# One product of 512 columns for the high part of a stationary weight tile, and the sum of its halves at the eviction

## The reference

```python
# first block: depthwise causal convolution over time (width 4) on 512 of the projected columns
qk = causal_dwconv(jnp.concatenate([mq, mk], axis=-1), conv_w[l], conv_b[l])
...
# first block, MLP (1024 -> 4096 -> 1024)
u = jnp.square(jax.nn.relu(h @ w_up[l]))
x = x + rmsnorm(u @ w_down[l], norm_mlp_post[l])
...
# second block, feed-forward of each of its two layers (1024 -> 2 x 2816 -> 1024)
def conv_ffn(h, w_up, conv_w, conv_b, w_down):
    u = h @ w_up
    up = jnp.pad(u, ((0, 0), (CONV_WIDTH_2 - 1, 0), (0, 0)))
    uc = conv_b + sum(conv_w[j] * up[:, j:j + S] for j in range(CONV_WIDTH_2))
    gate, val = uc[..., :D_FF_2], uc[..., D_FF_2:]
    return (jax.nn.silu(gate) * val) @ w_down
```

## Time and profile before

| | |
|---|---|
| median of 3 runs | 1218.11 us (1217.97 to 1219.54) |
| span of the profiled execution, first to last instruction | 1216.8 us |
| mean granted clock of PE in it | 0.973 |
| busy share of PE, PEld, DVE, ACT | 94%, 83%, 62%, 54% |
| weights and other data moved | 183.91 MB, mean 151 GB/s |

### The profile page before, as it was taken

The page is one execution under the profiler, slowest core; times in us unless marked ns, Lnnn a source line. Parts: engine busy times, 40 slices in busy tenths (PEclk is TensorE's granted clock), DMA queues, the critical chain, the costliest instruction groups (busy, mean ns, idle before and its releaser), DMA issues.

```text
span 1216.8 us, 19433 instructions
## 1 busy us (share of the span) xinstructions
PE 1144.5 (94%) x6808; PEld 1014.1 (83%) x6808; DVE 759.6 (62%) x1336; ACT 663.0 (54%) x1124; POOL 8.5 (1%) x11
## 2 busy tenths in 40 slices
PE   6998779999979999999999899999898988999998
PEld 4886678989968888988898799999787777999997
DVE  4667655555546766466654666776665745677666
ACT  5364454444456566465564655555655646555554
POOL 1000100000000000000000000000000000000000
PEclk9998789999999999999999999999999998999999
DMA  8552135666626554055622456555552514555562
GB/s 302 140 172 70 53 114 176 181 188 186 191 87 204 165 185 139 15 172 161 205 69 67 124 174 190 183 171 181 156 173 85 163 64 138 170 179 171 190 204 90
DMA packets 85283, 183.91 MB, mean 151 GB/s; under 512 B 6640, under 2 KB 6896, under 8 KB 84976
## 3 DMA queue, kind: packets, MB, share of 16 engines
q1 hardware_dynamic: 85232, 183.26, 48.2%
HBM read 182.19 MB, written 1.05 MB: 151 GB/s over the span
## 4 chain that ended last, share of the span: by engine, by line
PE 85%; DVE 6%; ACT 5%; issue 3%; DMA 0%; SPq 0%; DVEq 0%; ACTq 0%
PE ps L646 10%; PE ps L647 10%; PE ps L648 10%; PE ps L624 9%; PE ps L626 9%; PE ps L625 9%; PE ps L701 5%; PE ps L702 5%; PE ps L703 5%; PE ps L762 3%; PE ps L742 3%; PE ps L750 2%; DVE w_lo L1351 1%; ACT u L991 1%; PE ps L774 1%
## 5 line engine op out<-in xcount | busy, mean ns | idle before, releaser
L1351 DVE TENSOR_TENSOR w_lo<-w_stage,w_hi 128x1024 fp32r<-128x1024 f32 x336 | 404.1, 1222 | 263.7 <-ACT w_hi L967 263.6
L967 ACT ACTIVATE w_hi<-w_stage 128x1024 fp32r<-128x1024 f32 x336 | 350.0, 1057 | 323.4 <-PE ps L648 165.8
L646 PE MATMUL ps<-aT_hi,w_hi 128*128 128x256 f32 x992 | 285.5, 288 | 10.4 <-DVE aT_lo L1364 3.6
L647 PE MATMUL ps<-aT_lo,w_hi 128*128 128x256 f32 x992 | 284.2, 286 | 0.0
L648 PE MATMUL ps<-aT_hi,w_lo 128*128 128x256 f32 x992 | 284.1, 286 | 0.0
L624 PE MATMUL ps<-w_hi,aT_hi 128*128 128x512 f32 x512 | 205.8, 402 | 2.3 <-DVE aT_lo L1364 2.3
L646 PEld LDWEIGHTS ps<-aT_hi,w_hi 128*128 128x128 f32 x992 | 194.1, 196 | 14.3 <-issue 8.0
L626 PE MATMUL ps<-w_hi,aT_lo 128*128 128x512 f32 x512 | 202.4, 395 | 0.0
L625 PE MATMUL ps<-w_lo,aT_hi 128*128 128x512 f32 x512 | 202.2, 395 | 0.0
L647 PEld LDWEIGHTS ps<-aT_lo,w_hi 128*128 128x128 f32 x992 | 194.0, 196 | 1.0
L648 PEld LDWEIGHTS ps<-aT_hi,w_lo 128*128 128x128 f32 x992 | 193.9, 195 | 0.0
(11 more groups left out here) (173 smaller groups left out, 1151.4 us busy)
## 6 DMA issues: line engine op xcount, KB each, us to landing
w_stage<-in_ffn_w_up SPq DMA_DIRECT2D x88, 512.0 KB, 4.5
w_stage<-in_a_w_qkv SPq DMA_DIRECT2D x72, 512.0 KB, 4.3
w_stage<-in_ffn_w_down SPq DMA_DIRECT2D x44, 512.0 KB, 3.7
w_stage<-in_w_up SPq DMA_DIRECT2D x32, 512.0 KB, 4.3
w_stage<-in_w_down SPq DMA_DIRECT2D x32, 512.0 KB, 3.8
w_stage<-in_w_in SPq DMA_DIRECT2D x24, 512.0 KB, 4.4
w_stage<-in_b_w_qkv SPq DMA_DIRECT2D x24, 512.0 KB, 4.1
w_stage<-in_w_out SPq DMA_DIRECT2D x8, 512.0 KB, 4.0
```

What stands on the lines that cost most here:

```text
L646: pe.matmul(o, wh, aT_hi[:, k, :], start=(k == 0), stop=False)
L647: pe.matmul(o, wh, aT_lo[:, k, :], start=False, stop=False)
L967: act.activation(w_hi[:, slot, :], w_in[:, slot, :], ACT.Copy).then_inc(hi_done[slot], 1)
L1351: dve.tensor_tensor(w_lo[:, slot, :], w_in[:, slot, :], w_hi[:, slot, :].bitcast(F32), ALU.subtract).then_inc(lo_done[slot], 1)
```

## The change

`aT_hi` and `aT_lo` become the two halves of one tile, so that for a k tile the high and the low part of the activations lie side by side: 512 columns. In `dense_cols` the high part of a weight tile meets both in one product over the whole bank, and the low part meets the high activations in one product of 256 columns, into the first half of the bank. A new helper on DVE, `add_parts`, adds the two halves of the bank into `summed` (in `o_sb`, in SBUF) with a `tensor_reduce` over a view in which the pair is the innermost axis, and frees the bank. ACT's evictions and relus and DVE's shifted additions read `summed`; they wait for and count new semaphores (`conv`, `relu`). The cut diff:

```diff
-        aT_hi = sb("aT_hi", [P, KT, S], F32R)
-        aT_lo = sb("aT_lo", [P, KT, S], F32R)
+        aT = sb("aT", [P, KT, 2, S], F32R)
+        aT_hi, aT_lo = aT[:, :, 0, :], aT[:, :, 1, :]
...
+        summed = o_sb[:, 0, :].rearrange("p (f s) -> p f s", s=S)
...
-                            o = ps[:, bank(stg, names[f]), 0:S]
+                            o = ps[:, bank(stg, names[f]), :]
                             if k == 0:
                                 pe.wait_ge(*is_free(stg, names[f], i))
-                            pe.matmul(o, wh, aT_hi[:, k, :], start=(k == 0), stop=False)
-                            pe.matmul(o, wh, aT_lo[:, k, :], start=False, stop=False)
-                            last = pe.matmul(o, wl, aT_hi[:, k, :], start=False, stop=(k == KT - 1))
+                            both = aT[:, k, :, :].rearrange("p c s -> p (c s)")
+                            if k == 0:
+                                pe.matmul(o, wh, both, start=True, stop=False)
+                            last = pe.matmul(o[:, 0:S], wl, aT_hi[:, k, :], start=False, stop=False, skip_group_check=True)
+                            if k > 0:
+                                last = pe.matmul(o, wh, both, start=False, stop=(k == KT - 1))
...
+            def add_parts(stg, names, i, f):
+
+                dve.wait_ge(*is_full(stg, names[f], i))
+                dve.tensor_reduce(summed[:, f, :], ps[:, 4 + f, :].rearrange("p (c s) -> p s c", c=2), AX.X,
+                                  ALU.add).then_inc(drained[4 + f], 1)
...
             def relu_rows(stg, i, names, first):
                 for f in range(4):
-                    act.wait_ge(*is_full(stg, names[f], i))
-                    act.activation(hid[:, f, :], ps[:, 4 + f, 0:S], ACT.Relu).then_inc(drained[4 + f], 1)
+                    act.wait_ge(*is_drained(stg, names[f], i))
+                    act.activation(hid[:, f, :], summed[:, f, :], ACT.Relu).then_inc(s["relu"], 1)
...
             def square(stg, i, n, before):
 
                 for f in range(4):
-                    dve.wait_ge(*is_drained(stg, before[f], i))
+                    add_parts(stg, before, i, f)
+                dve.wait_ge(s["relu"], at(stg, "relu", 4 * n, i))
...
                 def convolve(stg, i, names, j, n):
 
                     for f in range(4):
+                        add_parts(stg, names, i, f)
+                    for f in range(4):
                         dve.wait_ge(s["cv"], at(stg, "cv", 4 * (n - 1) + f + 1, i))
                         for back in (1, 2):
                             sc = cw[:, bass.ds(j, 1), 4 * f + 2 - back:4 * f + 3 - back].rearrange("p a b -> p (a b)")
-                            ins_ = dve.scalar_tensor_tensor(out=hid[:, f, back:S], in0=ps[:, 4 + f, 0:S - back],
+                            ins_ = dve.scalar_tensor_tensor(out=hid[:, f, back:S], in0=summed[:, f, 0:S - back],
                                                             scalar=sc, in1=hid[:, f, back:S], op0=ALU.mult, op1=ALU.add)
```

More of the change, by code:

```diff
@@ L248, in ffn @@
     def ffn(tag):
[L250 removed]
+        up = {"cv": 4, "conv": 4, "silu": 1, "u": 1, "uhi": 1, "ulo": 1, "dve_step": 4}
         return [
@@ L260, in ffn @@
         ]
-    mlp_up = {"u": 1, "uhi": 1, "ulo": 1}
+    mlp_up = {"u": 1, "uhi": 1, "ulo": 1, "relu": 4}
     stages = [
@@ L377, in blocks_kernel @@
             "x_in0", "x_in1", "ident_in", "cols_in", "const_in", "gate_in", "stored", "ln_norm", "ln_post", "hiT", "mh", "ms", "rstd", "xn", "act_step", "dve_step",
-            "gates", "lnf", "rot", "cv", "ecv", "mqk", "sig", "gated", "prob", "pd", "oms", "wm",
-            "orstd", "osq", "sq", "ms8", "rs8", "silu", "u", "uhi", "ulo", "msq", "pms", "prstd", "x_new",
+            "gates", "lnf", "rot", "cv", "conv", "ecv", "mqk", "sig", "gated", "prob", "pd", "oms", "wm",
+            "orstd", "osq", "sq", "ms8", "rs8", "silu", "u", "uhi", "ulo", "relu", "msq", "pms", "prstd", "x_new",
             "lam", "const_ready", "gate_w", "unit")}
@@ L1111, in _ @@
             for f in range(4):
-                act.wait_ge(*is_full(S_, f"mqk{f}"))
-                act.activation(hid[:, f, :], ps[:, 4 + f, 0:S], ACT.Identity, scale=col("cw1", f * 4 + 3),
+                act.wait_ge(*is_drained(S_, f"mqk{f}"))
+                act.activation(hid[:, f, :], summed[:, f, :], ACT.Identity, scale=col("cw1", f * 4 + 3),
                                bias=col("cb1", f)).then_inc(s["cv"], 1)
@@ L1121, in _ @@
                            scale=-1.0).then_inc(drained[4], 1)
-            for f in range(4):
-                act.wait_ge(*is_drained(S_, f"mqk{f}"))
+            act.wait_ge(s["conv"], at(S_, "conv", 4))
             chain.link(act.activation(u32[:], hid[:].rearrange("p a b -> p (a b)"), ACT.Exp, scale=-1.0))
@@ L1261, in convolve @@
                     for f in range(4):
-                        act.wait_ge(*is_full(stg, names[f], i))
+                        act.wait_ge(*is_drained(stg, names[f], i))
                         sc = cw[:, bass.ds(j, 1), 4 * f + 2:4 * f + 3].rearrange("p a b -> p (a b)")
                         bi = cw[:, bass.ds(j, 1), 4 * f + 3:4 * f + 4].rearrange("p a b -> p (a b)")
-                        act.activation(hid[:, f, :], ps[:, 4 + f, 0:S], ACT.Identity, scale=sc, bias=bi).then_inc(s["cv"], 1)
-                    for f in range(2):
-                        act.wait_ge(*is_drained(stg, names[f], i))
+                        act.activation(hid[:, f, :], summed[:, f, :], ACT.Identity, scale=sc, bias=bi).then_inc(s["cv"], 1)
+                    act.wait_ge(s["conv"], at(stg, "conv", 4 * (n - 1) + 2, i))
                     act.activation(u32[:, W:2 * W], hid[:, 0:2, :].rearrange("p a b -> p (a b)"), ACT.Silu)\
```

11 lines of the change are left out of this document (5 added, 6 removed).

## The result

The changed kernel takes 1222.31 us, the median of 20 runs (1218.25 to 1226.07), against 1218.05 us, the median of 20 runs of the kernel before beside it (1216.43 to 1219.55). The ratio is 1.0034, with a 95% interval of 1.0024 to 1.0043. The forecast was 1215.5 us and faster; the kernel became slower by 4.3 us. The profiled execution has a span of 1217.5 us (1219.25 us with what lies around it), 0.7 us more than before, so it is one of the fastest of the twenty, where the profiled execution of the kernel before lies at its median.

The account below looks back on a forecast made before the run. PE was taken as the one bound, with DVE not far behind. Terms -12.8 + 4.5 + 2.5 + 2.2 - 2.7 - 3.0 + 2.6 + 3.8 = -2.9 us gave 1215.5 us, range 1209 to 1223.

Parts of the forecast that it names:

- products, 31 dense stages: PE's 992 groups, a pair replacing three products: 0.0129 us saved each, 12.8 us in all.
- ffn loops, PE behind `w_lo`: In 16 ffn loop stages, DVE's sums delay `w_lo`; 0.28 us a stage is given back, +4.5 us.
- `in1`, to the first product of `mv`: In `in1`, sums shift the splits behind the shifted additions by 2.4 us, restart adds 0.1: +2.5 us.
- head of the MLP, the wait: At the MLP's head, sums stand behind DVE's split, so PE gets the fourth bank later: +2.2 us.
- heads of the ffn, bank free earlier: At both ffn heads, sums free the bank before the additions: -1.35 us each, -2.7 together.
- heads of the ffn, clock stays high: At both ffn heads, PE's shorter waits keep its clock high: -3.0 us for both, 0 if not.
- tails of the ffn: At both ffn tails, sums delay `u_lo`, so PE resumes later: +1.3 us each, +2.6.
- lower clock behind the longer waits: In `in1`, the MLP's head and two tails: 60% of four times 1.6 us, +3.8 (0 to 6.4).
- the price of a pair: On PE, a 512-column and a 256-column product together cost 0.2269 + 0.1199 = 0.3468 us.
- a long ring through the landings: In the ffn loops, split, weight load, landing, ACT's rounding and next split set the period: 16.85 us taken.
- the ring through the transfer: Rival, ffn loops: later splits and late landings replace PE as the bound, period 17.15, time 1220 us; chance 0.25.
- the products don't gain: Rival, PE: cost goes with weights or bank switching, products save only 2.5 us, time 1221.5 us; chance 0.04.

Follow-up runs that it names:

- the base: Changed kernel with ACT copying the low half for DVE's addition, splits moved, and ACT's copies ahead of the MLP's fourth split: 1204.1 us, again 1203.52 us.

## Why the prediction was wrong, point by point

The terms of the sum, as forecast and as the profiled execution has them, in us. Each measured one is the distance between stage starts on PE, after minus before, with the products' saving taken out; the last but one is what is left of the span, nearly half of it ahead of the first `dense_cols` stage.

| term | forecast | measured |
|---|---|---|
| products, 31 dense stages | -12.8 | -8.0 |
| ffn loops, PE behind `w_lo` | +4.5 | +4.3 |
| `in1`, to the first product of `mv` | +2.5 | +2.3 |
| head of the MLP, the wait | +2.2 | +1.8 |
| heads of the ffn, bank free earlier | -2.7 | -2.6 |
| heads of the ffn, clock stays high | -3.0 | 0 |
| tails of the ffn | +2.6 | +2.4 |
| lower clock behind the longer waits | +3.8 | +2.7 |
| stretches without an edit | 0 | -2.2 |
| sum, in the span | -2.9 | +0.7 |

The forecast of 1215.5 is 6.8 us under the measured 1222.3. The sum in the span is 3.6 of that (-2.9 against +0.7), the step from the span to the median 3.5 (1.3 against 4.8), less 0.3 of rounding.

Of what is left in the stretches without an edit, 1.4 us lie around the MLP's tail, where the granted clock is 0.92 from 335 to 380 us against 0.89 before, and 0.9 behind ffn a's loop, where it is 1.00 from 862 to 885 us against 0.93, though PE's wait there had grown from 1.45 to 2.67 us. The 1.0 us ahead of the first stage has no such row beside it, and against all this 0.8 is lost between `in1` and the MLP and 0.2 behind the last stage.

**The step that failed first is the price of a pair.** The prediction took 0.2269 + 0.1199 = 0.3468 us, from rows in which products of one width follow one another. That holds in six stages; in the other 25 the alternation of 512 and 256 columns costs 0.3535, and 0.22 us a stage is saved, not 0.41. This is 4.8 us of the error. The forecast had the mechanism among its rivals (a cost that goes with switching between half a bank and a whole one), with a chance of 0.04 and a saving of 2.5 us; the measured one is a bit under two thirds of the forecast 12.8. Two products of a kind in a row bring 0.348 back, which speaks for the switching; that six stages alternate and have 0.347 all the same says that it isn't the whole of it. The nine traces in which the two kinds alternate in every stage say where the fast pace occurs. They hold 279 dense stages. In 136 of them PE runs into and through the stage with no wait and no change of clock (no pair starts more than 0.372 us behind the one before), and all 136 end at 0.3535. The fast pace stands only behind a pause or a change of clock: 64 of the other 143 end with it, 79 don't. So 0.3535 is the price for an undisturbed stream, and the six fast stages are those that a pause had happened to leave fast. The Trainium skill, "TensorE: Matmul & The Clock Gate", section "Wait — 56ns, not 53.3ns?", gives 2.5 ns as the fixed cost of a product. A product less in each of 992 groups brought 8.5 us, 8.6 ns each: neither the page's figure nor the 13 ns of the rows.

**The second is the clock at the heads of the ffn.** It was to stay high once PE's one wait became short, for 3.0 us. The two heads became 2.18 and 1.72 us shorter, and the products (1.3 in all) and the earlier bank (some 2.6) account for nearly all of it. The windows of the stages say why the clock gave nothing: stages A and B of head a and stage B of head b, first before, then after.

```profile
680.60:694.47 13.87, 13.16 (x96) 12.99 (x97) 9.65 (x15) 9.20 (x14) 0.00 (x0) 0.89 0.63 190
694.47:709.14 14.67, 13.86 (x97) 13.25 (x97) 8.86 (x13) 6.45 (x9) 0.00 (x0) 0.88 0.48 143
1034.88:1048.05 13.17, 12.37 (x96) 11.76 (x97) 8.85 (x13) 6.45 (x9) 0.00 (x0) 1.00 0.53 158
```

```profile
683.29:697.61 14.32, 13.98 (x65) 11.98 (x65) 9.29 (x14) 7.59 (x11) 0.00 (x0) 0.80 0.60 184
697.61:709.66 12.05, 12.05 (x65) 9.87 (x66) 11.39 (x18) 7.45 (x10) 0.00 (x0) 1.00 0.40 111
1035.92:1047.97 12.05, 12.05 (x65) 9.86 (x66) 11.39 (x18) 7.46 (x10) 0.00 (x0) 1.00 0.40 108
```

In head a the low clock of the earlier trace rows did go, 0.88 to 1.00 in stage B, about the 1.5 us of the forecast. But stage A, which has the same wait of 1.60 us ahead of it in both kernels, went from 0.89 to 0.80 and took most of it back. In head b there was nothing to win: its wait was as long, and the clock behind it was 1.00 already. The forecast had counted the row of one head twice. That the shorter wait is what kept the clock high in head a isn't shown either: with the products alone the wait was as long as before (0.74 us and three more) and the clock in stage B was 1.00 too.

**DVE's steps were right.** The sum has 681 ns (forecast 680), four of them 2.48 us, the additions 480 ns from SBUF against 479 from PSUM. The wait in the loop stands where it was put (in most stages of loop b it is too short for a row of its own and shows as a longer step at the second quarter) and gives back 8 x 0.37 + 8 x 0.17 = 4.3 us; the forecast had 4.5. But its form was half wrong. The forecast saw a long ring through the landings at 16.85 in both loops. What decides is DVE's own chain: with half the transfer the period moves by 0.14 and 0.02 us, with 1.0 us less on DVE by 0.37 and 0.17, and then PE doesn't wait. The Trainium skill, "VectorE: DVE Perf Modes", section "The TRN2 errata — SBUF-src ops pay a fixed extra latency per instruction", gives 120 cycles of fixed cost with the source in PSUM and 58 in SBUF. The rows of 480 ns (SBUF) and 479 (PSUM) don't show the 62 between them, as the forecast had it.

**`in1` and the tails** went as said. The first quarter of `mv` comes at 72.99, on DVE's splits that start at 71.71, and PE waited for it for 2.02 us; against the earlier trace rows, and with the stage before it 1.33 us ahead, this is +2.3. The tails' longer waits, +1.24 and +1.18, showed no drop of the clock in this profile.

```profile
71.71 4.62 DVE L1352 TENSOR_TENSOR w_lo<-w_stage,w_hi 128x1024 fp32r<-128x1024 f32 x4
```

```profile
72.99 0.50 PE L625 MATMUL ps<-w_hi,aT 128*128 128x512 f32 x1 [2.02 <-DVE w_lo L1352]
```

**The head of the MLP** cost 4.5 us, the clock's share in it: the wait itself 1.8 (the forecast's 2.2 was worked out at the fourth bank), and then stage B at the lower clock for 2.7 us more than before, the products' saving taken out. The forecast had spread its 3.8 us for the clock over four places with a weight of 60%; in this execution one place took 2.7 and the others nothing that can be seen.

**From the span to the median** there are 4.8 us (1217.5 and 1222.3), where the forecast put 1.3; 3.1 of them lie between the profiled execution and the median. So the terms in the table explain the profiled execution and not the median. The eleven runs with a mean clock of 0.972 or more have a mean of 1220.8 us, the nine with 0.969 or less 1224.1; the kernel before had 0.972 to 0.974 in all 43 runs of it that are listed with their clocks. So in most other runs the lower clock costs more than in the profiled one. The kernel with the narrow product first shows where it can fall. It has the same sums and the same median, and its profiled execution lies above it (1223.42 us, clock 0.971). Behind the wait in `in1` (2.04 us, here 2.02) its clock is 0.86 from 72 to 84 us, where the kernel after has 1.00, and behind the wait in ffn a's tail (2.60 us, here 2.67) it is 0.77 from 880 to 895 us, where the kernel after has 1.00 at the same place of the program. The forecast had named both places. That the drops follow the longer waits of PE is argued, not shown. For it: in the runs with the splits moved, with the low half by ACT and with both, the clocks are 0.972 to 0.977, and where the waits are longest (the sums alone), 0.965 to 0.968. Against it: with the products grouped they are 0.969 to 0.973 with nearly the waits of the base, and in the kernel before the clock fell behind a wait of 1.45 us where the kernel after, in its profile, kept it behind 2.67.

Of the rivals, the ring through the transfer gave 1220, near in the time but for another reason, and "the products don't gain" 1221.5, near in the time and half right in the reason. That either comes so close is luck: both leave the step from the span to the median at 1.3 us.

## What to carry to other kernels

Price a mixed stream by a mixed stream: a product's cost from rows of one width in a row was a best case for the stream here that alternates widths, and a small error there is multiplied by a thousand. When work moves onto an engine that stands ahead of the bound, look for the places where it stands behind a split that isn't urgent, or ahead of one that is; here two reorderings gave back 8.8 us, twice the loss, and half of each sum given to the less busy ACT some 9 more. A saving on the bound engine has arrived only when the median shows it: 3.3 us that the stages of a profile show went to the clock. And before a kernel is explained by its profile, look where the profiled execution lies among its runs: here 3.1 us under the median.

## What the runs showed that was not expected

- Alternating products of 512 and 256 columns run at one of two paces, 0.347 or 0.3535 us a pair. In nine traces it was 0.3535 in all of 136 stages without a disturbance, and 0.347 only behind a pause of PE or a change of its clock, in 64 of 143 stages. Both paces occur with and without sums, with whole and half transfers and in each order within the pair; two of a kind in a row give 0.348 in all stages of the loops. What decides behind a pause stays open.
- The granted clock can differ at a place where program and waits are the same: 1.00 or 0.86 at 868 to 880 us, in one and the same kernel on two occasions as well as between two kernels. It took back all of 3.3 us.
- A `tensor_reduce` whose inner axis is a pair 1 KB apart in PSUM costs what the other rows of 512 elements cost, 681 ns; a `tensor_tensor` of 256 elements, one half in PSUM and one in SBUF, takes 1.43 us for four.
